# Gate and up of the FFN as seven block products instead of eight, on one Trainium2 core

## The reference

```python
def swiglu(x, w_gate, w_up, w_down):
    return (jax.nn.silu(x @ w_gate) * (x @ w_up)) @ w_down
...
h = rms_norm(x, ffn1_norm[i])
x = x + 0.5 * swiglu(h, ffn1_w_gate[i], ffn1_w_up[i], ffn1_w_down[i])
h = rms_norm(x, mix_norm[i])
x = x + even_mixer(...)   # i = 0: a gated recurrence and block attention; i = 1: odd_mixer, a convolution and top-k attention
h = rms_norm(x, ffn2_norm[i])
x = x + 0.5 * swiglu(h, ffn2_w_gate[i], ffn2_w_up[i], ffn2_w_down[i])
```

## Time and profile before

| | |
|---|---|
| time, median of 3 runs | 1999.82 us (1998.88 to 1999.99) |
| the profiled execution's span | 1996.9 us |
| PE busy | 1968.5 us, 99% of the span |
| DVE, ACT, POOL busy | 54%, 39%, 3% |
| mean granted clock of PE | 0.997 |
| HBM read, written | 185.32 MB, 4.72 MB |

### The profile page before, as it was taken

The page is one execution under the profiler, slowest core; times in us unless marked ns, Lnnn a source line. Parts: engine busy times, 40 slices in busy tenths (PEclk is TensorE's granted clock), DMA queues, the critical chain, the costliest instruction groups (busy, mean ns, idle before and its releaser), DMA issues.

```text
span 1996.9 us, 25404 instructions
## 1 busy us (share of the span) xinstructions
PE 1968.5 (99%) x9054; PEld 1613.8 (81%) x9054; DVE 1076.8 (54%) x1673; ACT 771.1 (39%) x1110; POOL 50.0 (3%) x86
## 2 busy tenths in 40 slices
PE   7999999999999999999999999999999999999999
PEld 5888888888778888888888888877778778888887
DVE  5444444767674444446544444456989854444444
ACT  4222222477773222224332222354555852223222
POOL 1000000000000000000000000011111000000000
PEclk9999999999999999999999999999999999999999
DMA  4254433321122222233322233267765352332223
GB/s 166 101 122 121 137 96 100 110 74 64 55 84 95 95 95 96 99 100 105 106 95 95 95 96 102 96 163 168 158 153 133 87 137 96 97 103 95 95 95 105
DMA packets 60863, 213.80 MB, mean 107 GB/s; under 512 B 6616, under 2 KB 6872, under 8 KB 60792
## 3 DMA queue, kind: packets, MB, share of 16 engines
q1 hardware_dynamic: 52080, 184.97, 28.2%
q0 software_dynamic: 6192, 22.55, 6.2%
q10 hardware_dynamic: 2520, 5.36, 1.5%
HBM read 185.32 MB, written 4.72 MB: 95 GB/s over the span
## 4 chain that ended last, share of the span: by engine, by line
PE 89%; DVE 6%; ACT 3%; issue 2%; DMA 0%; SPq 0%; DVEq 0%; ACTq 0%
PE ps_unit L546 28%; PE ps_unit L548 28%; PE ps_unit L547 28%; DVE cv L1795 1%; DVE isc L1776 1%; PE ps_t L675 1%; DVE top L1774 1%; PE ps_s L546 1%; PE ps_y L547 0%; PE ps_y L548 0%; ACT w_hi L947 0%; PE ps_y L546 0%; PE ps_misc L636 0%; ACT L962 0%; DVE pt_lo L1543 0%
## 5 line engine op out<-in xcount | busy, mean ns | idle before, releaser
L947 ACT ACTIVATE w_hi<-raw 128x1024 fp32r<-128x1024 f32 x301 | 319.2, 1061 | 1019.9 <-PE ps_unit L548 1009.8
L546 PE MATMUL ps_unit<-xs_hi,w_hi 128*128 128x512 f32 x1768 | 697.3, 394 | 11.9 <-DVE xs_lo L1358 11.1
L547 PE MATMUL ps_unit<-xs_lo,w_hi 128*128 128x512 f32 x1768 | 688.9, 390 | 0.0
L548 PE MATMUL ps_unit<-xs_hi,w_lo 128*128 128x512 f32 x1696 | 660.9, 390 | 0.0
L1350 DVE TENSOR_TENSOR w_lo<-raw,w_hi 128x1024 fp32r<-128x1024 f32 x301 | 368.1, 1223 | 84.4 <-ACT w_hi L947 84.3
L546 PEld LDWEIGHTS ps_unit<-xs_hi,w_hi 128*128 128x128 f32 x1768 | 332.3, 188 | 87.8 <-DVE w_lo L1350 9.3
L547 PEld LDWEIGHTS ps_unit<-xs_lo,w_hi 128*128 128x128 f32 x1768 | 332.6, 188 | 68.5 <-issue 1.7
L548 PEld LDWEIGHTS ps_unit<-xs_hi,w_lo 128*128 128x128 f32 x1696 | 318.8, 188 | 66.9
L546 PE MATMUL ps_unit<-a_hi,w_hi 128*128 128x512 f32 x892 | 350.4, 393 | 2.4 <-DVE t L1472 0.8
L547 PE MATMUL ps_unit<-a_lo,w_hi 128*128 128x512 f32 x892 | 347.5, 390 | 0.0
L548 PE MATMUL ps_unit<-a_hi,w_lo 128*128 128x512 f32 x845 | 329.2, 390 | 0.0
(11 more groups left out here) (236 smaller groups left out, 1292.6 us busy)
## 6 DMA issues: line engine op xcount, KB each, us to landing
raw<-w_stream_dram SPq DMA_DIRECT2D x344, 512.0 KB, 3.5
w_lo<-raw POOLq DMA_DIRECT2D x28, 512.0 KB, 5.2
w_lo_3rd<-raw POOLq DMA_DIRECT2D x15, 512.0 KB, 5.3
skew<-table ACTq DMA_DIRECT2D x1, 2560.0 KB
bias_t<-skew ACTq DMA_DIRECT2D x1, 2048.0 KB, 9.7
out_dram<-xt SPq DMA_DIRECT2D x8, 256.0 KB, 2.0
xt<-xt_in_dram SPq DMA_DIRECT2D x7, 256.0 KB, 6.0
bd_raw<-bd_in_dram SPq DMA_DIRECT2D x1, 512.0 KB, 8.1
```

The lines of the kernel that those rows point to most:

```text
L546: pe.matmul(ps, lhs_hi, rhs_hi, start=first, stop=False)
L547: pe.matmul(ps, lhs_hi, rhs_lo, start=False, stop=False)
L548: return pe.matmul(ps, lhs_lo, rhs_hi, start=False, stop=last)
L947: act.activation(w_hi[:, s, :], raw[:, slot, :], ACT.Copy).then_inc(w_hi_done, 1)
```

## The change

Gate and up of a hidden tile are one product of a 2x2 block matrix (gate and up; even and odd tiles of x) with a 2x2 block matrix of x (even and odd tiles; first and second half of the tokens). It is done by the Strassen-Winograd scheme with **seven block products** instead of eight. A block product (`gu_product`) is four blocks x 3 matmuls of 128x256, so a tile is 84 matmuls of 256 columns instead of 48 of 512.

- **Weights.** A tile's gate and up weights arrive as four pieces of 128x512 in `gu` (`gu_load`, SP). Four sums of pieces are needed: the first and third come from POOL's accumulating DMAs (`sums`), the second and fourth from DVE (L1848, L1854). Seven pieces are split, by ACT into `gw_hi` and by DVE into `gw_lo` (L1839), in five steps of 1024 or 512 columns. `raw`, `w_hi`, `w_lo` carry the down units and the mixers as before.
- **Inputs.** From a pair of x tiles come seven operands of 256 tokens. `even_x` and `odd_x` make them with a subtraction and three dependent steps on DVE (L1762, L1774, L1776, L1778) and split them (L1766, L1783, L1786). Their scratch is one for all pairs, except that the first FFN has one per pair for its even tiles.
- **Results.** Products gather in a chain bank, which ACT copies out three times a tile (`chain_copy`), and in block banks; DVE forms gate (L1863), multiplies it by `rstd` (L1868), forms -up (L1878) and the product with silu (L1883). `half` becomes -0.5 of `rstd`.
- **Order.** A tile's products run 1, 5, 6, then the third of the tile before, 7, 4, 2. At a group's end (`ENDS`) the third product of the last tile stands between the first parts of down units 0 and 1, and the last tile's share of both comes behind; the next tile's last splits and fourth sum are made there.
- **Squares of x** are no longer made as tiles of x are finished, but in the first tile of the FFN (`squares_of_x`), each from the third on after an addition on DVE. The sum over partitions stands at that tile's end, the spreading of the diagonal behind product 6 of the second.
- **Loads.** `gu` lies where the mixers keep attention data: the next FFN's first two tiles are loaded when the last `weigh` is done. Between FFN and FFN they are loaded as the pieces come free.
- FFN loops are unrolled (PE's program grows from 5158 to 11843 instructions); the bias table is copied in nine parts instead of 128 and laid in 16 DMAs; `bd_raw` is loaded in the even phase and POOL clears the pads of v in the mixers.

```diff
--- before.py
+++ after.py
+ENDS = {GROUP_AT[g + 1] - 1: g for g in range(len(GROUPS)) if not SPREAD or g == len(GROUPS) - 1}
...
+def pended(j):
+    return j > 0 and j - 1 not in ENDS
...
+        _products = [(_f, 1), (_f, 5), (_f, 6), (_f - 1, 3), (_f, 7), (_f, 4), (_f, 2)] if pended(_j) else [(_f, p) for p in (1, 5, 6, 2, 7, 4)]
...
+        gu = sb("gu", [P, 11, PIECE])
+        gw_hi = sb("gw_hi", [P, 7, PIECE], F32R)
+        gw_lo = sb("gw_lo", [P, 7, PIECE], F32R)
...
+            def gu_load(f):
+                r = f % 2
+                if f >= 2 and f not in after_mixer:
+                    sp.wait_ge(sum_done, 2 * (f - 2) + 1)
+                    sp.wait_ge(gw_lo_done, split_count(f - 2, 0))
+                sp.dma_start(gu[:, 8 + r, :], gu_stream[f, 0][:, 1, :]).then_inc(gu_landed[r], 16)
+                if f >= 2 and f not in after_mixer:
+                    sp.wait_ge(sum_done, 2 * (f - 2) + 2)
+                    sp.wait_ge(gw_lo_done, split_count(f - 2, 3))
+                sp.wait_ge(gu_landed[r], 48 * (f // 2) + 16)
+                for part in range(2):
+                    sp.dma_start(gu[:, 4 * r + 2 * part:4 * r + 2 * part + 2, :], gu_stream[f, part]).then_inc(gu_landed[r], 16)
...
+                    sp.wait_ge(pv_done, 8 * (MIX_NO[i] + 1))
+                    for f in range(FFN_BASE[i + 1], FFN_BASE[i + 1] + 2):
+                        gu_load(f)
...
+            def sums(f):
+                r = f % 2
+                pool.wait_ge(gu_landed[r], 48 * (f // 2) + 16)
+                if f:
+                    pool.wait_ge(s1_landed, 16 * f)
+                pool.dma_start(gu[:, 8 + r, :], gu_stream[f, 1][:, 1, :], accum_op=ALU.add).then_inc(s1_landed, 16)
+                pool.wait_ge(gu_landed[r], 48 * (f // 2 + 1))
+                if f:
+                    pool.wait_ge(s3_landed, 16 * f)
...
+            def gu_product(ps, piece, hi, lo, first, wait=None):
+                for j in range(PAIRS):
+                    if wait:
+                        wait(j)
+                    w = slice(j * P, (j + 1) * P)
+                    pe.matmul(ps, gw_hi[:, piece, w], hi(j), start=first and j == 0, stop=False, skip_group_check=True)
+                    pe.matmul(ps, gw_hi[:, piece, w], lo(j), start=False, stop=False, skip_group_check=True)
+                    mm = pe.matmul(ps, gw_lo[:, piece, w], hi(j), start=False, stop=j == PAIRS - 1, skip_group_check=True)
...
+                def a12_u2():
+                    pe.wait_ge(gw_lo_done, split_count(f, 3))
+                    gu_product(block_bank(r, 0), 5, *of_u(1, 0), True, landed(ub_done))
...
+                gu_product(chain, 0, *of_u(0, 0), True, landed(ua_done))
...
+                gu_product(block_bank(r, 2), 1, *of_u(0, 1), True)
...
+                gu_product(chain, 2, *of_xu(1), False, landed(uc_done))
...
+                if more:
+                    gate_right(f - 1)
+                else:
+                    a12_u2()
...
+                gu_product(chain, 3, *of_xu(0), False)
+                gu_product(block_bank(r, 1), 4, *of_xu(2), False)
+                if more:
+                    a12_u2()
+                if first:
+                    pe.wait_ge(const_done, 2)
+                    pe.wait_ge(acc_done, KT * (i + 1))
+                    for t in range(TT):
...
+            def gate_right(f):
+                pe.wait_ge(gw_lo_done, split_count(f, 4))
+                pe.wait_ge(up_done, f + 1)
...
+                    if j in ENDS:
+                        g, u0 = ENDS[j], ENDS[j] * KT
+                        before = GROUPS[g] - 1
+                        start_unit(UNIT_BASE[i] + u0, is_first=UNIT_BASE[i] + u0 < 2)
+                        down_part(i, u0, range(before))
+                        gate_right(f)
+                        start_unit(UNIT_BASE[i] + u0 + 1, is_first=UNIT_BASE[i] + u0 + 1 < 2)
+                        down_part(i, u0 + 1, range(before))
+                        for u in (u0, u0 + 1):
+                            down_part(i, u, [before]).then_inc(unit_done, 1)
+                        for u in range(u0 + 2, u0 + KT):
+                            down_unit(i, u)
...
+            def squares_of_x(i):
+                act.wait_ge(ua_done, PAIRS * (FFN_NO[i] + 1))
+                act.wait_ge(uc_done, PAIRS * (FFN_NO[i] + 1))
+                for d in range(KT):
+                    if d >= 2:
+                        act.wait_ge(acc_done, i * KT + max(2, d - 1))
+                    act.activation((t0, t1)[d % 2][:, :], xt_tile(d), ACT.Square).then_inc(sq_done, 1)
...
+            def even_x(i, j):
+                dve.tensor_tensor(s[:, 1, :], s[:, 2, :], s[:, 0, :], ALU.subtract).then_inc(u5_done, 1)
...
+                dve.tensor_tensor(xs_lo[:, 2 * j, :].rearrange("p (h t) -> p h t", t=TH), scr_even(i, j)[:, 0:2, :],
+                                  xs_hi[:, 2 * j, :].rearrange("p (h t) -> p h t", t=TH).bitcast(F32), ALU.subtract).then_inc(ua_done, 1)
+            def odd_x(i, j):
...
+                dve.scalar_tensor_tensor(scr[:, 3, :], x[:, TH:T], g, s[:, 2, :], ALU.mult, ALU.subtract).then_inc(u76_done, 1)
+                dve.wait_ge(u76_done, 2 * n - 1)
+                dve.scalar_tensor_tensor(scr[:, 4, :], scr[:, 3, :], -1.0, s[:, 0, :], ALU.mult, ALU.subtract).then_inc(u76_done, 1)
+                dve.wait_ge(u76_done, 2 * n)
+                dve.scalar_tensor_tensor(scr[:, 5, :], x[:, 0:TH], g, scr[:, 4, :], ALU.mult, ALU.add).then_inc(u4_done, 1)
...
+                dve.scalar_tensor_tensor(xs_lo[:, 2 * j + 1, :], xt_tile(2 * j + 1), minus(i * KT + 2 * j + 1),
...
+                dve.tensor_tensor(xu_lo[:, j, :].rearrange("p (h t) -> p h t", t=TH), scr[:, 3:6, :],
...
+            def second_sum(f):
+                r = f % 2
+                dve.wait_ge(s1_landed, 16 * (f + 1))
+                dve.wait_ge(gu_landed[r], 48 * (f // 2 + 1))
+                if f:
+                    dve.wait_ge(gw_lo_done, split_count(f - 1, 4))
...
+            def gate(f):
+                r = f % 2
+                dve.wait_ge(prod_done, prod_count(f, 3))
+                dve.wait_ge(copy_done, 3 * f + 2)
+                if f:
+                    dve.wait_ge(silu_done, f)
+                dve.tensor_tensor(t0[:, :].rearrange("p (h t) -> p h t", t=TH), sqb[:, r, :].rearrange("p (h t) -> p h t", t=TH),
...
+                            next_x(i + 1, e)
+                            for k in GW_AFTER.get(e, ()):
+                                gw_low(FFN_BASE[i + 1], k)
+                                if k == 0:
+                                    second_sum(FFN_BASE[i + 1])
+                                if k == 1:
```

765 lines of the change are left out of this document (543 added, 222 removed).

## The result

The change takes 2049.75 us (2048.44 to 2053.51) against 1999.64, a ratio of 1.0253 (1.0239 to 1.0268): **50 us slower**, where 2014 was forecast and 2040 was the end of the range.

What follows compares the result with a forecast made beforehand. PE, busy 99% of the span, was taken as the bound. Terms -94.5 + 31 + 27.8 + 20.2 + 18.1 + 8.0 + 4 = +14.6 on the 1999.8 median gave 2014 us, range 1978 to 2040.

Steps and rivals of the forecast that it cites:

- Products: PE's gate and up matmuls: a tile goes from 10.88 to 9.80 us, -94.5 us over 88 tiles.
- The tile loop on DVE: DVE's work per tile, about 8.5 us back to back, stays under PE's 9.80, so PE never waits.
- Rivals C and D: C: handovers bind the tile loop, 2032 to 2039, chance 0.17. D: 256-column matmuls take 0.125 us, 2075, chance 0.05.
- E: POOL's accumulating DMAs, two a tile in series, make sums late by 0.6 us a tile: +53, 2067; chance 0.05.
- Group ends: Unit 2 waits for its weight split: 2.3 us at eight ends, 3.2 at four, together +31 us.
- small parts: Bias table in fewer copies, `bd_raw`, pads: beside PE's work, some 2 us if cover goes; longer program 0, up to 5.
- Start: First FFN: product 6 begins near 40 us, tile 1 ends near 63; 27.8 us lost.
- Even mixer: Joint from even mixer to FFN: product 6 at 615 us, behind x operands and splits; 20.2 us lost.
- odd mixer: Joint from odd mixer to FFN: same as the even one with additions spread otherwise; 18.1 us lost.
- FFN to FFN: Joint between FFNs: eight units leave room for three pairs; last pair, squares and diagonal remain, 8.0 us lost.
- Clock: PE's waits at four places may each bring a few microseconds at half pace: +4 us, between 0 and 10.
- Rival B: Joints and group ends cost only DVE's own work, handovers hidden: 1979, or 1986 with half the group ends' share; chance 0.33.

Runs made afterwards that it cites:

- staggered run: Changed kernel, at group ends third product after three tiles of unit 0, then unit 0's rest interleaved with unit 1's first tiles: 2018.9 us.
- the first run: Changed kernel, SP issues the third tile's gate and up loads before a group's last down-unit loads: 2038.2 us, ratio 1.0196.
- the second run: Changed kernel, the bias table's 16 DMAs issued by POOL two tiles after the second group's start instead of by ACT: 2077.0 us.
- four mends: Changed kernel with third-tile loads earlier on SP, units 0 and 1 staggered, sum over partitions later, bias DMAs in pairs on ACT: 1990.9 us, ratio 0.9957.

## Why the prediction was wrong

**Products, right.** 9.76 us a tile against 9.80, so -98 us instead of -94.5. The earlier trace rows was the right row: nine matmuls stood for 7392. The Trainium skill gives about 109 ns for an isolated matmul of 256 columns at the full clock ("TensorE: Matmul & The Clock Gate", "Back-to-back issue gap"). By an estimate from this figure a tile would take 9.2 us. The trace after shows 9.76 (116 ns each, every matmul with a weight load), so here too the measurement decides.

**The tile loop on DVE, right.** No wait inside the loop, at 36 of 40 us busy. Rivals C and D did not occur. E's sign, sums that come late, occurred only behind groups and behind the odd mixer, and not for E's reason: the loads under them, or POOL's issue of them, were late.

**Group ends, right in mechanism and size, short of what followed.** Against the pace of the earlier trace rows, 2.3 us at eight tiles as forecast where the clock held (2.6 at the first), 3.9 at the three where it fell; 3.2 at six tiles, 3.9 at two of these (at one of them without two later waits of 1 us, which are counted at its joint). Together 37 us instead of 31. The staggered run shows the mechanism.

**The step that failed** is in the part on the tile loop and in the small parts: "are covered". The sum gave transfers and their issue nothing. I costed transfers by duration and bandwidth and never followed SP's queue through a group's end, where eight loads wait for splits and a later tile's stand behind them. It cost 16.8 us, shown by the first run. I named rival E for POOL's sums and gave it 0.05; its place was one queue further up. In the same way the bias table was "beside PE's work" because its copies were fewer; the issues stand on ACT ahead of a split: 5.9 us, shown by the second run. The two are 22.7 of the 35 us between the +14.6 worked out and the +49.8 measured.

**Inputs of an FFN.** Start: 63.35 against 63.1. Even mixer: 21 us against 20.2 and 1 of clock. Two were too small: odd mixer 24 instead of 19, FFN to FFN 16 instead of 9 (each with its 1 us of clock; taken from the marks of PE's timeline at the phase before and at the second tile's end, in both kernels, with 18.2 us of matmuls for two tiles now and 21.8 before).

The first two agree in part by luck. At the start I had two down splits of 2.4 us on DVE ahead of product 6; DVE makes them after its last operand, and two splits on ACT hold the copy instead. Behind the mixers I expected PE idle for 13 to 16 us before product 6, ended by `xu_lo`. It waits 1.3 and 2.6 us there. At the even mixer the rest lies in its last units (2.8 and 1.2 us for `w_lo`), in product 1 (4.8 us for `xs_lo`) and before the sum, 13.6 us in all where 20 were worked out, and matmuls slower than the paces of the earlier trace rows make up some 6. The total came out, the path did not.

The trace puts the odd mixer's 5 us more down to the late sum, 4.11 us of DVE's stream. That the loads "have 9 us, which suffices" was worked out for the even mixer, and the odd one was taken as the same. No run moved that sum; with four mends DVE still waits 4.3 us there. For FFN to FFN I gave eight units of 4.1 us room for three pairs. Per unit DVE has an addition and a scaling (1.4), a split (1.0), half a pair (2.1) and its share of the first tile's weights (0.7), together 5.2 us. That is more than a unit, and the earlier trace rows would have said so; it is a sum from rows that no run tests. The squares' wait, taken as 3.8 us, was 2.2 to 3.5, and taking them out gave 5.2.

The 0.15 us for a dependent step of DVE was a misreading of the earlier trace rows. In the kernel before, 64 of the 96 scalings of down units are followed by their addition after about 0.15 us, all in the rolled groups of eight; in the unrolled last groups it is 0.03 to 0.04, as in all 96 after the change. Two such steps in a pair made the chain 0.3 us too long.

**Clock.** 4 us was taken. It isn't measured apart; the slow matmuls grew by some 35 us of the run, of which a part lies where PE would have waited anyway. They are 6.5 to 9.1 us at each of the four joints, so 4 was too little; at the even mixer what was too much in the waits made up for it. In the ends of groups the clock shows alone: 1.6 us behind some of the waits.

The account: -98 (products) + 28 (start) + 21 (even mixer) + 24 (odd mixer) + 16 (FFN to FFN) + 37 (group ends) + 6 (bias table) + 17 (SP's queue) = 51 us, measured 49.8 between the two spans. The sign was right. Rival B's price was not: joints and group ends cost 126 us, where it had under 87. The last three runs, which moved steps of x and the third copy, moved waits between ACT and DVE and gained no more than 2 us.

## What to carry to other kernels

Where loads wait in one queue, write down for each place what stands ahead of each load and when that is released; a load's own duration says nothing of when it starts. A product that is cheaper on TensorE is paid at the joints: count them (here 4 FFN starts, 12 group ends), and weigh their sum against the gain before the loop. The mends show how near the two were: 59 us lay in the order of the same instructions, and the scheme then wins by 8.5. Take the cost of a handover between dependent instructions from code of the same form: the rolled loop's was some four times the unrolled one's here.

## What the runs showed of the hardware

- The same wait of 2 us, before the same instructions, was followed by a mean granted clock of 0.82 over 8 us in one place and of 1.00 in another; three of seven ends behind eight tiles took the 1.6 us more.
- Fourteen DMAs for the bias table, issued one behind the other, take ACT 0.45 us each (6.30 us), in another run 0.63 each (8.84 us), and ACT computes nothing meanwhile. Issued by POOL, the sixteen held its queue from 185.9 to 223.2 us, 27 of it in two pauses between issues.
- Dependent steps of DVE follow each other with 0.03 to 0.04 us between them, at 256 columns and at 512, where the program is unrolled. In the rolled loops of the kernel before, the same two steps on 512 columns are about 0.15 us apart.
- 256-column matmuls with a weight load each follow each other every 116 ns over whole tiles (84 in 9.76 us), at a granted clock of 1.00.
- An accumulating DMA of 256 KB from DRAM lands 5.4 us after its issue in the median, and once, behind the odd mixer, 9.2 us after.
